# A transformer-style block on one core: the last chunk of the output projection and half of the first gate chunk done one token tile after the other

## The chip, the core and the metric

One core of a Trainium2 chip runs the whole kernel. The metric is the device time of one execution in microseconds (us), taken as the median of several runs. The engines are TensorE (PE in the rows, PEld for its weight loads), VectorE (DVE), ScalarE (ACT), GpSimd (POOL) and SyncE (SP, which here only issues transfers). L and a number is a line of the kernel.

## What is computed

One layer of a block with batch 1, 256 tokens and D_MODEL = 2048, all in float32. Three token mixers (a short gated convolution, a differential attention, a cross attention into 256 memory tokens) give `merged`; then follows what matters here:

```
x = x + rmsnorm(merged @ w_o, g_mix_post)          # w_o 2048 x 2048
h = rmsnorm(x, g_ffn_pre)
u = causal_dwconv(h @ w_up, ffn_conv_w)            # w_up 2048 x 11264
gate, val = split(u, 2)
x = x + rmsnorm((silu(gate) * val) @ w_down, g_ffn_post)
```

`rmsnorm(x, g) = x * rsqrt(mean(x*x) + 1e-6) * g`, with the mean over the 2048 channels of a token.

## The kernel before, in words

**Weights in blocks.** The 256 tokens are two token tiles of 128 (NT = 2, t = 0 and 1). All weights stream in blocks of 256 rows by 512 columns (512 KB, KB = 2 slices of 128 rows); a chunk is 512 output columns and takes CB = 8 blocks when the inner dimension is 2048. SyncE loads a block into one of RING = 4 buffers `raw`. To keep float32 accuracy each block is split in two `float32r` parts: ScalarE writes `w_hi` (a rounded copy, `split`, L434), VectorE writes `w_lo` = raw - w_hi (L696), both in rings of four. SyncE may reload a `raw` buffer when the low part of the block that was in it is written (`lo_ready`); ScalarE may overwrite a `w_hi` when TensorE has finished with the block in it (`block_done`).

**The output projection.** Four chunks of 512 columns (NCH = 4). For each block TensorE does `multiply` (L1061 to L1063): for each of 2 slices and each of 2 token tiles three matmuls of 512 columns (hi·hi, hi·lo, lo·hi), 12 in all. The tokens are the stationary side, the weights move. A chunk fills two PSUM banks, one for each token tile; `ACC[0]` is banks 0 and 1, `ACC[1]` banks 2 and 3, and the last chunk uses `ACC[1]`.

**Between the projections.** When the last chunk is done, ScalarE squares it (`mix_squares`, L598), VectorE adds the sums of squares (L970) and multiplies by the gain (`mix_out`, L915), GpSimd forms r_mix (L381, L384), VectorE writes the new x (L980) in four groups g of 512 channels, both token tiles in a group, and TensorE transposes each group (`turn`, L1075, eight transposes 128x128). From PSUM ScalarE writes `h2_hi` (L443) and VectorE `h2_lo` (L704); the two lie side by side in `h2_pair`, which the rows name hT_pair. ScalarE squares the new x (L646) for the second norm. That norm's factor is not applied to h but to the columns of the up projection: it is spread over a row of 256 tokens by two matmuls (L1261, `r_row`) and multiplied in afterwards.

**The up projection.** Eleven steps, each a gate chunk (PSUM banks 0 to 3) and a value chunk (banks 4 to 7). Here the weights are stationary and the tokens move. For each block `multiply_up` does 2 slices x 4 column blocks x 2 matmuls: L1241 multiplies a 128x128 piece of w_hi with [h2_hi | h2_lo], 512 columns, and L1243 the same piece of w_lo with h2_hi, 256 columns.

Every engine's order is written out by hand, and each runs its own list; semaphores tie them. The order around the change on ScalarE is in `up_step` (L633 to L651), on VectorE in `new_x` and `up_step` (L967 to L1009), on TensorE in L1222 to L1277.

## Time and profile before

| | |
|---|---|
| median of 3 runs | 1710.1 us (1707.93 to 1711.38) |
| time of the profiled execution | 1701.58 us |
| span of its instructions | 1699.8 us |
| mean granted TensorE clock | 0.994 |
| busy: PE, PEld, DVE, ACT, POOL | 1673.2, 1408.2, 1004.0, 799.2, 21.4 us |
| bytes moved, mean rate | 320.89 MB, 189 GB/s |

All times below are from the one profiled execution. Its time is 8.5 us under the median of the runs. A matmul's recorded duration contains its way through the array, and matmuls overlap, so the cost of one in a row of them is the distance between starts, not its duration.

### The profile page before, as it was taken

How to read it: one execution, taken by the hardware profiler on the slowest of the kernel's cores; microseconds unless marked ns; L12 is line 12 of the kernel's file. 1: busy time of each engine (PE TensorE's matmuls, PEld its weight loads, DVE VectorE, ACT ScalarE, POOL GpSimd, SP SyncE). 2: the span in 40 equal slices, each digit the busy share in tenths (PEclk: the TensorE clock that was granted, in tenths of full speed). 3: DMA queues.
4: the chain of work that ended last, by engine and by line, in shares of the span. 5: the costliest groups of instructions: out<-in, count | busy, mean ns of one | idle time of the engine just before them, and what ended most of it. 6: DMA issues, size and time to landing. Idle time of an engine off the chain costs nothing.

```text
span 1699.8 us, 23037 instructions
## 1 busy us (share of the span) xinstructions
PE 1673.2 (98%) x8201; PEld 1408.2 (83%) x8201; DVE 1004.0 (59%) x1148; ACT 799.2 (47%) x1006; POOL 21.4 (1%) x49
## 2 busy tenths in 40 slices
PE   8999999999999999999999899999999999999997
PEld 7888888888888888888888688888888888888886
DVE  5554555544556656665555567777777777644544
ACT  5544444444444444444444455555555555443442
POOL 0000000000000000000000000000000000000000
PEclk9999999999999999999999899999999999999999
DMA  7666555666655655575655356666666566655653
GB/s 275 203 177 185 170 159 163 186 187 185 191 183 194 236 184 180 179 233 193 198 191 188 119 177 193 190 187 196 186 195 187 184 183 188 234 190 170 210 198 123
DMA packets 165791, 320.89 MB, mean 189 GB/s; under 512 B 10520, under 2 KB 11369, under 8 KB 165225
## 3 DMA queue, kind: packets, MB, share of 16 engines
q1 hardware_dynamic: 165705, 320.15, 59.7%
q8 instruction: 35, 0.57, 0.1%
q14 instruction: 19, 0.16, 0.0%
q10 hardware_dynamic: 32, 0.01, 0.0%
HBM read 318.02 MB, written 2.10 MB: 188 GB/s over the span
## 4 chain that ended last, share of the span: by engine, by line
PE 95%; DVE 3%; ACT 1%; issue 1%; DMA 0%; DVEq 0%; SPq 0%; ACTq 0%
PE PS L1241 19%; PE PS L1061 18%; PE PS L1063 18%; PE PS L1062 18%; PE PS L1243 10%; PE PS L1213 3%; PE PS L1212 3%; PE PS L1211 3%; PE PS L1075 1%; ACT w_hi L434 0%; PE PS L1153 0%; PE PS L1138 0%; DMA mem_sb<-in_mem_dram 0%; DVE y_down L1043 0%; ACT p_diff L565 0%
## 5 line engine op out<-in xcount | busy, mean ns | idle before, releaser
L696 DVE TENSOR_TENSOR w_lo<-raw,w_hi 128x1024 fp32r<-128x1024 f32 x583 | 709.4, 1224 | 632.0 <-ACT w_hi L434 629.5
L434 ACT ACTIVATE w_hi<-raw 128x1024 fp32r<-128x1024 f32 x583 | 609.6, 1057 | 627.1 <-PE PS L1063 507.7
L1241 PE MATMUL PS<-hT_pair,w_hi 128*128 128x512 f32 x1408 | 489.7, 392 | 0.0
L1243 PE MATMUL PS<-hT_pair,w_lo 128*128 128x256 f32 x1408 | 394.6, 280 | 0.0
L1061 PE MATMUL PS<-w_hi,hT_pair 128*128 128x512 f32 x832 | 329.5, 396 | 0.0
L1063 PE MATMUL PS<-w_hi,hT_pair 128*128 128x512 f32 x832 | 324.3, 390 | 0.0
L1062 PE MATMUL PS<-w_lo,hT_pair 128*128 128x512 f32 x832 | 323.9, 389 | 0.0
L1241 PEld LDWEIGHTS PS<-hT_pair,w_hi 128*128 128x128 f32 x1408 | 264.0, 188 | 58.2 <-issue 0.3
L1243 PEld LDWEIGHTS PS<-hT_pair,w_lo 128*128 128x128 f32 x1408 | 266.6, 189 | 0.0
L1061 PEld LDWEIGHTS PS<-w_hi,hT_pair 128*128 128x128 f32 x832 | 156.3, 188 | 33.6 <-issue 2.7
L1063 PEld LDWEIGHTS PS<-w_hi,hT_pair 128*128 128x128 f32 x832 | 156.2, 188 | 33.1
L1062 PEld LDWEIGHTS PS<-w_lo,hT_pair 128*128 128x128 f32 x832 | 156.4, 188 | 31.3
L1061 PE MATMUL PS<-w_hi,act_hi 128*128 128x512 f32 x352 | 137.2, 390 | 0.0
L1063 PE MATMUL PS<-w_hi,act_lo 128*128 128x512 f32 x352 | 137.0, 389 | 0.0
L1062 PE MATMUL PS<-w_lo,act_hi 128*128 128x512 f32 x352 | 136.9, 389 | 0.0
L1061 PEld LDWEIGHTS PS<-w_hi,act_hi 128*128 128x128 f32 x352 | 66.1, 188 | 14.4 <-issue 0.6
L1063 PEld LDWEIGHTS PS<-w_hi,act_lo 128*128 128x128 f32 x352 | 66.1, 188 | 13.7
L1062 PEld LDWEIGHTS PS<-w_lo,act_hi 128*128 128x128 f32 x352 | 66.1, 188 | 13.6
L1061 PE MATMUL PS<-w_hi,memT_hi 128*128 128x512 f32 x128 | 51.2, 400 | 1.0 <-DVE up_taps L726 0.7
L1063 PE MATMUL PS<-w_hi,memT_lo 128*128 128x512 f32 x128 | 50.2, 392 | 0.0
L1062 PE MATMUL PS<-w_lo,memT_hi 128*128 128x512 f32 x128 | 50.2, 392 | 0.0
L1061 PE MATMUL PS<-w_hi,mixT_hi 128*128 128x512 f32 x128 | 49.9, 390 | 0.0
(185 smaller groups left out, 1280.4 us busy)
## 6 DMA issues: line engine op xcount, KB each, us to landing
raw<-in_w_up_dram SPq DMA_DIRECT2D x176, 512.0 KB, 3.8
raw<-in_w_in_dram SPq DMA_DIRECT2D x112, 512.0 KB, 3.7
raw<-in_w_gate_dram SPq DMA_DIRECT2D x96, 512.0 KB, 3.9
raw<-in_w_down_dram SPq DMA_DIRECT2D x88, 512.0 KB, 4.1
raw<-in_w_mem_kv_dram SPq DMA_DIRECT2D x32, 512.0 KB, 4.0
raw<-in_w_o_dram SPq DMA_DIRECT2D x32, 512.0 KB, 3.6
raw<-in_w_conv_out_dram SPq DMA_DIRECT2D x16, 512.0 KB, 3.6
raw<-in_w_cross_out_dram SPq DMA_DIRECT2D x16, 512.0 KB, 3.8
```

Of the source, the lines that this page charges most:

```text
L434: nc.scalar.activation(w_hi[i % RING][:], raw[i % RING][:], ACT.Copy).then_inc(hi_ready, inc)
L696: nc.vector.tensor_tensor(w_lo[i % RING][:], raw[i % RING][:], w_hi[i % RING][:].bitcast(F32), ALU.subtract).then_inc(lo_ready, inc)
L1061: nc.tensor.matmul(o, a_hi, b_hi, start=first, stop=False)
L1062: nc.tensor.matmul(o, a_hi, b_lo, start=False, stop=False)
L1063: last = nc.tensor.matmul(o, a_lo, b_hi, start=False, stop=last_k)
L1075: last = nc.tensor.transpose(dst[:, b, t * P:(t + 1) * P], src[:, t, b * P:(b + 1) * P], ident[:])
L1211: nc.tensor.matmul(ACC[1][:, t, :], hi[:, k, s], w_hi[i % RING][:, c, :], start=k == 0, stop=False)
L1212: nc.tensor.matmul(ACC[1][:, t, :], hi[:, k, s], w_lo[i % RING][:, c, :], start=False, stop=False)
L1213: last = nc.tensor.matmul(ACC[1][:, t, :], lo[:, k, s], w_hi[i % RING][:, c, :], start=False, stop=k == HK - 1)
L1241: nc.tensor.matmul(o.rearrange("p (a t) -> p a t", a=2), b_hi, h2_pair[:, :, k, :], start=k == 0, stop=False, skip_group_check=True)
L1243: last = nc.tensor.matmul(o[:, 0:TOK], b_lo, h2_hi[:, k, :], start=False, stop=last_k, skip_group_check=True)
```

## The change

The last chunk of the output projection keeps all its eight blocks (`kept_hi`, `kept_lo`: four new buffers each beside the ring of four), and TensorE goes through them twice: first all blocks for token tile 0, then all for token tile 1. Squares, gain, r_mix, the new x, its transposes and the hi/lo halves of h2 are done for one token tile at a time. The eight pieces are listed in MID as (t, g), and each has one PSUM bank of its own out of banks 4 to 7. The first gate chunk of the up projection also keeps its eight blocks. Its blocks 0 to 3 (SPLIT = 4) are multiplied for token tile 0 (column blocks 0 to 2 first, since bank 3 still holds the output projection's tile 1) and later for token tile 1; blocks 4 to 7 for both together as before. Transposes stand between those pieces.

```diff
+SPLIT = 4
+MID = [(0, 0), (0, 1), (1, 0), (1, 1), (0, 2), (1, 2), (0, 3), (1, 3)]
...
+        kept_hi = [at(f"kept_hi{s}", RD + 16 * K + 4 * K * s, [P, KB, CW], F32R) for s in range(RING)] + w_hi
+        kept_lo = [at(f"kept_lo{s}", RD + 44 * K + 4 * K * s, [P, KB, CW], F32R) for s in range(RING)] + w_lo
...
+        MID_T = [PS[:, 4 + p % 4, :].rearrange("p (b t) -> p b t", t=P) for p in range(len(MID))]
...
-            pool.wait_ge(mix_sum, 1)
-            rms(r_mix[:], sq_mix[:], D)
+            for t in range(NT):
+                pool.wait_ge(mix_sum, t + 1)
+                rms(r_mix[:, t:t + 1], sq_mix[:, t:t + 1], D, 1)
...
+            def split_kept(n, i, fresh=False):
+                act.wait_ge(raw_in[i % RING], 4 * n + 16 * (i // RING + 1))
+                if not (fresh and i < RING):
+                    act.wait_ge(block_done, n + i - 2 * RING + 1)
+                nc.scalar.activation(kept_hi[i][:], raw[i % RING][:], ACT.Copy).then_inc(hi_ready, 1)
...
+            def last_squares(t):
+                if t == 0:
+                    act.wait_ge(o_first, 1)
+                else:
+                    act.wait_ge(block_done, N_UP)
+                act.wait_ge(mix_sq, NT * (NCH - 1) + 2 * t)
+                nc.scalar.activation(junk[:], ACC[1][:, t, :], ACT.Square, accum_out=sq_part[:, t, NCH - 1:NCH]).then_inc(mix_sq, 1)
+            def new_squares(t):
+                act.wait_ge(x_new, NCH * (t + 1))
+                act.wait_ge(mix_sq, NT * (NCH - 1) + 1 + 2 * t)
+                nc.scalar.activation(junk_wide[:], x_res[:, t, :], ACT.Square, accum_out=sq_h2[:, t:t + 1]).then_inc(mix_sq, 1)
+            def middle_hi(p):
+                t, g = MID[p]
+                act.wait_ge(mid_turned, p + 1)
+                for b in range(BPC):
+                    k = BPC * g + b
+                    last = nc.scalar.activation(h2_hi[:, k, t * P:(t + 1) * P], MID_T[p][:, b, :], ACT.Copy, scale=g_ffn_v[:, k:k + 1])
+                last.then_inc(mid_hi, 1)
+            def middle():
+                last_squares(0)
+                split_kept(N_UP, 0)
+                split_kept(N_UP, 1)
+                split_kept(N_UP, 2)
+                middle_hi(0)
+                split_kept(N_UP, 3)
+                middle_hi(1)
+                split_kept(N_UP, 4)
+                split_kept(N_UP, 5)
+                new_squares(0)
+                last_squares(1)
+                split_kept(N_UP, 6)
+                middle_hi(2)
+                middle_hi(3)
+                split_kept(N_UP, 7)
+                for p in range(4, 8):
+                    middle_hi(p)
+                new_squares(1)
+                act.wait_ge(r_row_turned, 1)
+                nc.scalar.activation(r_row[:], PS[:, 4, 0:TOK], ACT.Copy).then_inc(r_row_done, 1)
...
+            def last_out(t):
+                s = slice((NCH - 1) * CW, NCH * CW)
+                dve.wait_ge(mix_sq, NT * (NCH - 1) + 1 + 2 * t)
+                nc.vector.tensor_reduce(sq_mix[:, t:t + 1], sq_part[:, t, :], AX.X, ALU.add).then_inc(mix_sum, 1)
+                nc.vector.tensor_tensor(y_mix[:, t, s], ACC[1][:, t, :], g_post[:, s], ALU.mult).then_inc(mix_last, 1)
+            def new_x(t, g):
+                if g == 0:
+                    dve.wait_ge(mix_last, t + 1)
+                    dve.wait_ge(xres_in, 16 * NT)
+                    dve.wait_ge(rms_ready, 3 + t)
+                s = slice(g * CW, (g + 1) * CW)
+                nc.vector.scalar_tensor_tensor(out=x_res[:, t, s], in0=y_mix[:, t, s], scalar=r_mix[:, t:t + 1],
+                                               in1=x_res[:, t, s], op0=ALU.mult, op1=ALU.add).then_inc(x_new, 1)
+            def middle_lo(p):
+                t, g = MID[p]
+                dve.wait_ge(mid_hi, p + 1)
+                for b in range(BPC):
+                    k, s = BPC * g + b, slice(t * P, (t + 1) * P)
+                    last = nc.vector.scalar_tensor_tensor(out=h2_lo[:, k, s], in0=MID_T[p][:, b, :], scalar=g_ffn_v[:, k:k + 1],
+                                                          in1=h2_hi[:, k, s].bitcast(F32), op0=ALU.mult, op1=ALU.subtract)
+                last.then_inc(mid_lo, 1)
+            def middle():
                 dve.wait_ge(evacuated[0], E_UP)
-                dve.wait_ge(xres_in, 16 * NT)
-                dve.wait_ge(rms_ready, 3)
-                for g in range(NCH + 1):
-                    if g < NCH:
-                        s = slice(g * CW, (g + 1) * CW)
-                        for t in range(NT):
-                            last = nc.vector.scalar_tensor_tensor(out=x_res[:, t, s], in0=y_mix[:, t, s], scalar=r_mix[:, t:t + 1],
-                                                                  in1=x_res[:, t, s], op0=ALU.mult, op1=ALU.add)
-                        last.then_inc(x_new, 1)
-                    if g:
-                        prepare(2 * NCH + g - 1, g - 1, (SCORE_T, TURN)[(g - 1) % 2], g_ffn_v, h2_hi, h2_lo)
+                dve.wait_ge(evacuated[1], E_UP - 1)
+                last_out(0)
+                new_x(0, 0)
+                new_x(0, 1)
+                split_kept(N_UP, 0)
+                split_kept(N_UP, 1)
+                middle_lo(0)
+                new_x(0, 2)
+                new_x(0, 3)
+                split_kept(N_UP, 2)
+                middle_lo(1)
+                split_kept(N_UP, 3)
+                last_out(1)
+                split_kept(N_UP, 4)
+                new_x(1, 0)
+                new_x(1, 1)
+                split_kept(N_UP, 5)
+                middle_lo(2)
+                middle_lo(3)
+                new_x(1, 2)
+                new_x(1, 3)
+                split_kept(N_UP, 6)
+                middle_lo(4)
+                middle_lo(5)
+                split_kept(N_UP, 7)
+                middle_lo(6)
+                middle_lo(7)
                 dve.wait_ge(mix_sq, NT * NCH + NT)
                 nc.vector.tensor_copy(sq_mix[:], sq_h2[:]).then_inc(h2_sq, 1)
+                dve.wait_ge(rms_ready, 5)
+                nc.vector.memset(ones[:], 1.0)
+                for t in range(NT):
+                    last = nc.vector.tensor_scalar(r_diag[:, t, :], ident[:], r_h2[:, t:t + 1], None, ALU.mult)
+                last.then_inc(r_diag_done, 1)
...
+            def middle_turn(p):
+                t, g = MID[p]
+                if p == 0:
+                    pe.wait_ge(turned_read, T_UP)
+                if p >= 4:
+                    pe.wait_ge(mid_lo, p - 3)
+                pe.wait_ge(x_new, NCH * t + g + 1)
+                for b in range(BPC):
+                    c0 = (BPC * g + b) * P
+                    last = nc.tensor.transpose(MID_T[p][:, b, :], x_res[:, t, c0:c0 + P], ident[:])
+                last.then_inc(mid_turned, 1)
+            def last_chunk():
+                n, acc = N_O + CB * (NCH - 1), ACC[1]
+                pe.wait_ge(evacuated[1], E_O + 1)
+                for t in range(NT):
+                    s = slice(t * P, (t + 1) * P)
+                    for i in range(CB):
+                        if t == 0:
+                            pe.wait_ge(lo_ready, n + i + 1)
+                        for c in range(KB):
+                            k = KB * i + c
+                            b_hi, b_lo = kept_hi[i][:, c, :], kept_lo[i][:, c, :]
+                            nc.tensor.matmul(acc[:, t, :], mixT_hi[:, k, s], b_hi, start=k == 0, stop=False)
+                            nc.tensor.matmul(acc[:, t, :], mixT_hi[:, k, s], b_lo, start=False, stop=False)
+                            last = nc.tensor.matmul(acc[:, t, :], mixT_lo[:, k, s], b_hi, start=False, stop=k == DK - 1)
+                        if t:
+                            last.then_inc(block_done, 1)
+                        elif i == CB - 1:
+                            last.then_inc(o_first, 1)
+                        if t and i in (3, 4):
+                            middle_turn(i - 3)
+            def first_gate():
+                def tile(i, t, blocks):
+                    s = slice(t * P, (t + 1) * P)
+                    for c in range(KB):
+                        k = KB * i + c
+                        for b in blocks:
+                            w = slice(b * P, (b + 1) * P)
+                            o = UP[0][:, b, :].rearrange("p (a t) -> p a t", a=2)
+                            nc.tensor.matmul(o[:, :, s], kept_hi[i][:, c, w], h2_pair[:, :, k, s], start=k == 0 and t == 0, stop=False,
+                                             skip_group_check=True)
+                            last = nc.tensor.matmul(o[:, 0, s], kept_lo[i][:, c, w], h2_hi[:, k, s], start=False, stop=False,
+                                                    skip_group_check=True)
+                    return last
+                pe.wait_ge(evacuated[0], E_UP)
+                pe.wait_ge(mix_last, 1)
+                for i in range(SPLIT):
+                    pe.wait_ge(mid_lo, i // 2 + 1)
+                    pe.wait_ge(lo_ready, N_UP + i + 1)
+                    tile(i, 0, range(BPC - 1))
+                    if i >= 2:
+                        middle_turn(i)
+                pe.wait_ge(mix_last, 2)
+                for i in range(SPLIT):
+                    tile(i, 0, range(BPC - 1, BPC))
+                middle_turn(4)
+                for i in range(SPLIT):
+                    pe.wait_ge(mid_lo, 2 + i // 2 + 1)
+                    tile(i, 1, range(BPC)).then_inc(block_done, 1)
+                    if i < 3:
+                        middle_turn(5 + i)
+                for i in range(SPLIT, CB):
+                    pe.wait_ge(mid_lo, 6 if i // 2 == 2 else 8)
+                    multiply_up(N_UP, i, 0, kept_hi[i], kept_lo[i])
+                    if i == CB - 2:
+                        spread_scale()
```

Beside this the squares and gain product of the third output chunk come two blocks later in the last chunk (after block 5, not 3), and `new_x`, `prepare` and the transposes of before are gone from this stage. How the orders differ:

TensorE, around the end of the output projection. Before, all transposes of the new x (x_res) stand together behind the last output matmul (L1063) and ahead of the first up matmul (L1241); the names in brackets are the semaphores waited for:

```order
L1063 MATMUL PS<-w_hi3_56,mixT_lo_102 128x512
L1075 MATMUL PS<-ident_61,x_res_106 128x128 [waits x_new]
L1075 MATMUL PS<-ident_61,x_res_106 128x128 x7
L1075 MATMUL PS<-ident_61,x_res_106 128x128 [waits x_new,turned_read]
L1075 MATMUL PS<-ident_61,x_res_106 128x128 x7
L1075 MATMUL PS<-ident_61,x_res_106 128x128 [waits x_new,prep_lo]
L1075 MATMUL PS<-ident_61,x_res_106 128x128 x7
L1075 MATMUL PS<-ident_61,x_res_106 128x128 [waits x_new,prep_lo,turned_read]
L1075 MATMUL PS<-ident_61,x_res_106 128x128 x7
L1241 MATMUL PS<-hT_pair_92,w_hi0_53 128x512 [waits prep_lo,lo_ready,evacuated1,evacuated0]
```

In the changed kernel the third piece of transposes, which is token tile 1's first, stands between block 2 and block 3 of the gate chunk; L1363 is the hi matmul of one token tile (2x128 columns), L1365 the lo matmul (128 columns):

```order
L1363 MATMUL PS<-hT_pair_92,kept_hi2_140 128x2x128
L1365 MATMUL PS<-hT_pair_92,kept_lo2_144 128x128
L1329 MATMUL PS<-ident_61,x_res_106 128x128 [waits x_new]
L1329 MATMUL PS<-ident_61,x_res_106 128x128 x3
L1363 MATMUL PS<-hT_pair_92,kept_hi3_141 128x2x128 [waits lo_ready,mid_lo]
L1365 MATMUL PS<-hT_pair_92,kept_lo3_145 128x128
```

What moved: 32 transposes that stood in one place are eight pieces of four among matmuls, and a 512/256 pair of columns has become two pairs of 256/128.

ScalarE, the same stage before, from the squares of the last chunk to the next splits of weights:

```order
L598 ACTIVATE junk_137,sq_part_78<-PS 128x512 [waits mix_sq,block_done]
L598 ACTIVATE junk_137,sq_part_78<-PS 128x512 [waits mix_sq]
L443 ACTIVATE hT_pair_92<-PS,vecs_63 128x256 [waits prep_turned]
L443 ACTIVATE hT_pair_92<-PS,vecs_63 128x256 x3
L443 ACTIVATE hT_pair_92<-PS,vecs_63 128x256 [waits prep_turned]
L443 ACTIVATE hT_pair_92<-PS,vecs_63 128x256 x3
```

ScalarE in the changed kernel, from block 3 of the gate chunk on (L614 splits a block, L648 writes a piece of h2_hi, L640 squares the whole new x of token tile 0, L634 squares the last chunk of token tile 1):

```order
L614 ACTIVATE kept_hi3_141<-raw3_52 128x1024 [waits block_done,raw_in3]
L648 ACTIVATE hT_pair_92<-PS,vecs_63 128x128 [waits mid_turned]
L648 ACTIVATE hT_pair_92<-PS,vecs_63 128x128 x3
L614 ACTIVATE w_hi0_53<-raw0_49 128x1024 [waits block_done,raw_in0]
L614 ACTIVATE w_hi1_54<-raw1_50 128x1024 [waits block_done,raw_in1]
L640 ACTIVATE junk_wide_146,sq_h2_80<-x_res_106 128x2048 [waits mix_sq,x_new]
L634 ACTIVATE junk_137,sq_part_78<-PS 128x512 [waits mix_sq,block_done]
L614 ACTIVATE w_hi2_55<-raw2_51 128x1024 [waits block_done,raw_in2]
```

What moved: token tile 1's squares (L634) now stand behind five weight splits and the long squares of token tile 0.

VectorE in the changed kernel, from token tile 1's sum of squares to its transposed halves (L1032 adds the sums, L1033 multiplies by the gain, L965 writes a low part of weights, L1042 writes a group of the new x, L1051 a piece of h2_lo):

```order
L1032 TENSOR_REDUCE sq_mix_79<-sq_part_78 128x1 [waits mix_sq]
L1033 TENSOR_TENSOR y_mix_110<-PS,g_post_117 128x512
L965 TENSOR_TENSOR w_lo0_57<-raw0_49,w_hi0_53 128x1024 [waits hi_ready]
L1042 SCALAR_TENSOR_TENSOR x_res_106<-y_mix_110,r_mix_75,x_res_106 128x512 [waits rms_ready,xres_in,mix_last]
L1042 SCALAR_TENSOR_TENSOR x_res_106<-y_mix_110,r_mix_75,x_res_106 128x512
L965 TENSOR_TENSOR w_lo1_58<-raw1_50,w_hi1_54 128x1024 [waits hi_ready]
```

Before, the same place holds all of the last chunk at once, and no weights:

```order
L970 TENSOR_REDUCE sq_mix_79<-sq_part_78 128x2 [waits mix_sq]
L915 TENSOR_TENSOR y_mix_110<-PS,g_post_117 128x512 [waits mix_sq]
L915 TENSOR_TENSOR y_mix_110<-PS,g_post_117 128x512
L980 SCALAR_TENSOR_TENSOR x_res_106<-y_mix_110,r_mix_75,x_res_106 128x512 [waits xres_in,rms_ready,evacuated0,evacuated1]
L980 SCALAR_TENSOR_TENSOR x_res_106<-y_mix_110,r_mix_75,x_res_106 128x512 x3
```

What moved: a weight's low part now stands between the gain product and the new x of token tile 1.

## Rows read from the trace of the kernel before

**Rows 1.** The page's first part: busy time of TensorE and its share of the span.
```profile
PE 1673.2 (98%) x8201; PEld 1408.2 (83%) x8201; DVE 1004.0 (59%) x1148; ACT 799.2 (47%) x1006; POOL 21.4 (1%) x49
```
**Rows 2.** Stretches between the projections: busy PE, PEld, DVE, ACT, POOL, then PEclk, DMA share, GB/s.
```profile
944.00:948.00 4.00, 0.04 (x1) 0.00 (x0) 2.45 (x5) 1.38 (x4) 0.88 (x2) 1.00 0.51 155
948.00:951.00 3.00, 2.62 (x13) 2.62 (x14) 1.65 (x3) 0.62 (x2) 0.00 (x0) 0.50 0.00 0
951.00:954.50 3.50, 0.90 (x6) 0.70 (x6) 3.25 (x7) 2.41 (x7) 0.00 (x0) 0.95 0.00 0
958.00:961.50 3.50, 3.50 (x14) 3.11 (x13) 2.08 (x6) 2.25 (x5) 0.00 (x0) 0.50 0.02 5
962.00:966.00 4.00, 4.00 (x25) 3.48 (x25) 0.30 (x2) 3.94 (x6) 0.81 (x2) 1.00 0.00 0
```
**Rows 3.** TensorE in order of time: start us, us, line, [idle before it <- releaser].
```profile
943.65 0.39 PE L1063 MATMUL PS<-w_hi,mixT_lo 128*128 128x512 f32 x1
...
948.38 3.41 PE L1075 MATMUL PS<-ident,x_res 128*128 128x128 f32 x16 [4.34 <-DVE x_res L980]
...
954.38 1.57 PE L1075 MATMUL PS<-ident,x_res 128*128 128x128 f32 x8 [2.60 <-DVE x_res L980]
...
957.27 1.94 PE L1075 MATMUL PS<-ident,x_res 128*128 128x128 f32 x8 [1.32 <-DVE x_res L980]
...
958.86 0.77 PE L1241 MATMUL PS<-hT_pair,w_hi 128*128 128x512 f32 x1
...
959.65 0.63 PE L1241 MATMUL PS<-hT_pair,w_hi 128*128 128x512 f32 x1
...
960.29 0.63 PE L1241 MATMUL PS<-hT_pair,w_hi 128*128 128x512 f32 x1
```
**Rows 4.** TensorE at full clock: transposes, the scale's matmuls, up pairs, first value matmul.
```profile
861.39 1.03 PE L1075 MATMUL PS<-ident,stage 128*128 128x128 f32 x8
...
979.63 0.60 PE L1261 MATMUL PS<-r_diag,ones 128*128 128x128 f32 x4
...
980.77 0.39 PE L1241 MATMUL PS<-hT_pair,w_hi 128*128 128x512 f32 x1
981.00 0.28 PE L1243 MATMUL PS<-hT_pair,w_lo 128*128 128x256 f32 x1
981.12 0.39 PE L1241 MATMUL PS<-hT_pair,w_hi 128*128 128x512 f32 x1
...
983.01 0.47 PE L1241 MATMUL PS<-hT_pair,w_hi 128*128 128x512 f32 x1
```
**Rows 5.** Output projection by tile: durations ns min/median/max, first and last start us.
```profile
L1061 PE MATMUL PS<-w_hi,mixT_hi x128: 389/389/476, 855.9 to 943.2; 128*128 128x512 f32 x128
```
**Rows 6.** The other engines between the projections, in order of time.
```profile
944.07 0.60 ACT L598 ACTIVATE junk<-PS 128x512 f32<-128x512 f32 x1 [1.60 <-PE PS L1063]
...
945.51 0.16 DVE L970 TENSOR_REDUCE sq_mix<-sq_part 128x2 f32<-128x8 f32 x1 [1.78 <-ACT junk L598]
945.59 1.28 DVE L915 TENSOR_TENSOR y_mix<-PS,g_post 128x512 f32<-128x512 f32 x2
...
946.04 0.69 POOL L384 TENSOR_TENSOR r_mix<-mean_sq,minus_half 128x2 f32<-128x2 f32 x1
946.91 2.74 DVE L980 SCALAR_TENSOR_TENSOR x_res<-y_mix,r_mix,x_res 128x512 f32<-128x512 f32 x4
...
954.15 1.65 DVE L704 SCALAR_TENSOR_TENSOR hT_pair<-PS,vecs,hT_pair 128x256 fp32r<-128x256 f32 x4
...
955.99 1.57 ACT L443 ACTIVATE hT_pair<-PS,vecs 128x256 fp32r<-128x256 f32 x4 [2.58 <-PE PS L1075]
...
960.69 1.93 ACT L646 ACTIVATE junk_wide<-x_res 128x2048 f32<-128x2048 f32 x1
...
964.78 2.96 ACT L434 ACTIVATE w_hi<-raw 128x1024 fp32r<-128x1024 f32 x3
...
965.87 2.36 DVE L696 TENSOR_TENSOR w_lo<-raw,w_hi 128x1024 fp32r<-128x1024 f32 x2 [0.92 <-ACT w_hi L434]
```
**Rows 7.** DMA issues: size and median us from issue to landing.
```profile
raw<-in_w_up_dram SPq DMA_DIRECT2D x176, 512.0 KB, 3.8
```

109 lines of the change are left out of this document (45 added, 64 removed).

## The prediction

> **What bounds the kernel now.** I read the page first. TensorE is busy 98% of the span [rows 1], so time can only come from the places where it stands still or runs slowly. I then cut the span into stretches and looked for those where PE's busy time or its granted clock drops. One such place lies where this change is made: in 944 to 948 us TensorE is busy 0.04 us of 4.00, in 948 to 951 us and again in 958 to 961.5 us its clock is 0.50 (1.2 GHz instead of 2.4), and from 962 us on it is full again [rows 2].
>
> The time order says why. The last output matmul starts at 943.65, the first transposes at 948.38 after 4.34 us idle, and two more waits of 2.60 and 1.32 us follow, all three released by VectorE's new x (L980); the first up matmul starts at 958.86 [rows 3]. Behind the 4.34 us stands a chain over all engines: squares at 944.07, sum at 945.51, gain product at 945.59, r_mix at 946.04, new x from 946.91 [rows 6].
>
> How much is lost there? At full clock:
> - an output matmul costs 0.2275 us. From the first L1061 at 855.9 to the last at 943.2 there are 127 steps of three, with eight transposes (0.9 us) among them: (87.3 - 0.9) / 381 = 0.227 [rows 5];
> - an up pair of 512 and 256 columns costs 0.348 us: two starts at 980.77 and 981.12, of which the 512-column one takes 0.23 and the 256-column one 0.115 [rows 4];
> - a transpose costs (1.03 - 0.27) / 7 = 0.109 us, if 0.27 is one's own duration, and each of the four records that the two scale matmuls leave (0.60 - 0.27) / 3 = 0.11, so 0.22 a matmul [rows 4].
>
> From the end of the last output matmul, 943.65 + 0.23 = 943.88, to the first value matmul at 983.01 [rows 3, 4] it is 39.1 us. The work in it is 64 pairs (22.25), 32 transposes (3.5) and the two scale matmuls (0.4), 26.1 us. So **13.0 us are lost**: 8.3 waiting, and 4.7 since most transposes and the first four pairs ran at half clock (a pair then takes 0.64, 959.65 to 960.29 [rows 3]). 13.0 us is 0.8% of the kernel and the most that this change can give.
>
> **The change part by part.** All sums count from the end of the last output matmul of token tile 0, or of both.
>
> *The output chunk in two passes.* 96 matmuls of 512 columns before and after: 0. The second pass (48 matmuls, 10.9 us, with two pieces of transposes between, 11.9) is what covers tile 0's chain. That its blocks are all there in the first pass needs eight blocks held: four go to new buffers without waiting for TensorE, so they are split during the third chunk; nothing waits. With that cover gone a block would cost the landing time, 3.8 us [rows 7].
>
> *Tile 0's chain.* Durations come from the rows of before, halved where one token tile is done: squares to +0.9 us, sum +1.0, gain product (half of 1.28) +1.65, r_mix +2.1, first new x (2.74 / 4 = 0.69) +2.9 [rows 6]. TensorE asks for it after four blocks of the second pass, 24 x 0.2275 = +5.5. Hidden with 2.6 us to spare. h2's first piece: transposes done at +6.1, four ScalarE copies, four VectorE operations. Of 128 columns I have no row. 256 columns take 1.57 / 4 = 0.39 on ScalarE and 1.65 / 4 = 0.41 on VectorE [rows 6]. The slope from there to 1024 columns on ScalarE (2.96 / 3 = 0.99) and to 512 on VectorE (0.69) gives 0.29 and 0.28 for 128; the upper bound is no saving at all. So the piece is ready at +8.5 and TensorE wants it at +11.9. Hidden. Thus the 4.34 us wait goes completely.
>
> *Tile 1's chain: here is the one wait left.* Let 0 be the end of the first pass, so tile 1 is done at 11.9. Its squares could start at 12.1, but on ScalarE they stand behind the splits of blocks 3, 4 and 5 (0.99 each), two pieces of copies (1.2 each) and the squares of the whole tile 0 (2.07 with its read-out). In order: first piece 6.1 to 7.3, block 3 to 8.3, second piece to 9.4, blocks 4 and 5 to 11.4, long squares to 13.5, tile 1's squares to 14.2. The raw blocks 4 and 5 are asked for at 5.0 and 6.2 and land 3.8 us later [rows 7], in time. VectorE then has the sum (0.1), the gain product (0.64), the low part of block 4 (2.36 / 2 = 1.18), and the first new x (0.69): 16.9. TensorE has three blocks of three column pieces to do from 11.9, 18 narrow pairs. At 0.231 a pair (below) that is 4.16, to 16.05. It waits **0.9 us**, for VectorE's x_res. The next thing that can be late is the third group of tile 1's new x, needed at 23.5 and there at 22.5, so nothing. The last pieces (hi7, lo7) are done 10 us before blocks 6 and 7 need them, and the second norm's factor 4 us before the scale matmuls.
>
> *Narrow matmuls: the cost that the change adds.* Blocks 0 to 3 took 32 pairs of 512/256 columns; now they are 64 pairs of 256/128. If cost went by columns this would be free. But each pair loads its two weights again. 256 columns cost 0.115. For 128 columns of this type the trace has no row. The bounds: 0.057, half of 256; and 0.22, what a plain float32 matmul of 128 columns costs in its two records [rows 4]. I take **0.115, the same as 256 columns**: no two starts with a weight load between them are nearer than 0.109 in these rows. Then 64 x 0.231 = 14.8 against 32 x 0.348 = 11.1: **+3.65 us**. The ends: 64 x 0.173 = 11.1 (+0, but then TensorE asks 1.05 us earlier and waits that much longer, so +1), and 64 x 0.335 = 21.4 (+10.3, and the wait of 0.9 is gone).
>
> The Trainium skill has two rules here (TensorE: Matmul & The Clock Gate). Its section on the back-to-back gap gives a lone 128-column matmul N / 2.4 + 2.5, about 56 ns, the low end; its section on LDWEIGHTS gives a weight load of 128 columns about 107 ns whatever the contraction. By the first alone the sum would be some 2.7 us better, by the second 0.5 better. The 0.109 of the rows speaks for the second, but comes from another type of matmul.
>
> *Transposes.* 32 before and after, at full clock 3.5 us. Eight places instead of four, and after eight transposes the next matmul starts in the rows about 0.05 late; 8 x 0.05 = +0.4.
>
> *The end of the stage.* The value chunk's first block still cannot be split before the row of scales is read by ScalarE, as before; that small stop is inside the 39.1 us, and I allow 0.1 us for it again. More loops, semaphores and GpSimd's two small norms instead of one are beside other work.
>
> **The sum.** 26.1 + 3.65 + 0.4 + 0.9 + 0.1 = 31.1 us instead of 39.1: **8.0 us less**. The profiled execution would go from 1701.6 to 1693.6; against the median of 1710.1 that is **1702.1 us** (-0.47%). What can be told from no change here is about 0.2%, 3.4 us.
>
> **The rivals.**
> 1. *128-column float32r matmuls cost as much as plain float32, 0.22.* For it: plain float32 is the only 128-column multiplication in the trace, and it costs that. Against it: 256 and 512 columns of this type cost in proportion to their columns, so the type by itself is not slow. The stage is then 26.1 + 10.3 + 0.4 + 0.1 = 36.9, so 2.2 us less, 1707.9: within 0.2%.
> 2. *The chains are longer than my slopes.* If 128 columns cost ScalarE and VectorE what 256 do, the wait at tile 1's first transposes grows from 0.9 to 1.8 us and a small one of 0.1 follows; gain 7.0, 1703.1. Landings 3 us late on top would put blocks 4 and 5, which stand ahead of the squares on ScalarE, late by about as much: gain 4 to 5, still faster.
> 3. *Slower: the clock falls and stays at 1.2 GHz through the tiled stretch.* The stretch has a wait of 0.9 us, transposes in eight places and narrow matmuls. At half clock a narrow pair costs 0.21 + 0.21, if 128 columns again go like a transpose of that stretch (3.41 us for 16 with three at the end faster [rows 3], 0.21 each): 64 x 0.43 = 27.3 instead of 14.8, and six pieces of transposes 2.5 more, less the wait: +14. That is 6 us slower than before, 1716. It decides once the half clock covers more than 8/14 of some 18 us, so 10 us. Against it: the clock was still 1.00 over the 4 us without work, 944 to 948, and fell only behind them [rows 2]; a wait of 0.9 us is far from that. The skill says (same page, PE-mode transpose) that transposes do not count as activity for the full clock. That rule would be this rival's reason. The rows say otherwise: 948 to 951 us holds nothing but transposes at 0.50, and 951 to 954.5 us stands at 0.95 [rows 2].
>
> **How the numbers follow.** My forecast, with rival 2 as its own upper part, 0.68 (of this rival 2 is 0.12): gain 4 to 10, that is 1700 to 1706. Rival 1: 0.21, 1706.5 to 1709. Rival 3: 0.06. The rest, 0.05, is some wait I have not seen, of either sign. The low end takes the gain of 10 with narrow pairs at 0.173 and 1 us of scatter between runs (the three of before lie 3.5 apart): 1699. The high end has to reach into rival 1 to hold 8 in 10: 1708.5. Faster by over 0.2%: 0.71; within 0.2%: 0.22; slower by over 0.2%: 0.07.
>
> **What the profile after would show.** The 4.34 us wait is gone, and the largest left on TensorE in this stage is about 0.9 us, before the transposes of token tile 1's first group, released by x_res. The distance between two starts of L1363 is 0.23; 0.17 or 0.33 would show my price for 128 columns wrong. The clock stays at 1.00 from the output projection into the up projection. From the first matmul of the last output chunk to the first value matmul it takes 53 us (before: 21.8 + 39.1 = 60.9). If these hold and the time doesn't fall, a later stage has given the gain back, which I see no reason for: from the first value chunk on the order is the same and TensorE sets the pace. I am wrong above all if the narrow pairs take over 0.30 us, or if TensorE shows a second wait of over 2 us.

## The result, and the profile after

| | before | changed |
|---|---|---|
| median | 1709.77 us (1707.93 to 1711.38, 4 executions) | 1692.06 us (1691.04 to 1692.9, 4 executions) |
| profiled execution | 1701.58 us | 1691.04 us |
| span | 1699.8 us | 1689.2 us |
| mean granted TensorE clock | 0.994 | 0.998 |

The ratio is 0.9911, 95% interval 0.9884 to 0.9937: 17.7 us less. The forecast was 8.0 us less, at 1702.1 us, and its range ended at 1699.0. So the time is outside the range. Already here two numbers don't fit each other: between the medians there are 17.7 us, between the profiled executions 10.5. The kernel before's profiled execution, 1701.58, is none of its four timed ones and lies over 6 us under the lowest of them.

The page's first part of the changed kernel, which answers to [rows 1]:

```profile
PE 1670.8 (99%) x8265; PEld 1408.2 (83%) x8265; DVE 1005.0 (59%) x1165; ACT 801.4 (47%) x1022; POOL 22.0 (1%) x51
```

Stretches of the changed kernel between the projections (us, busy PE, PEld, DVE, ACT, POOL, then PEclk, DMA share, GB/s), against [rows 2]:

```profile
930.00:942.00 12.00, 12.00 (x59) 9.94 (x58) 8.36 (x15) 8.72 (x16) 0.74 (x2) 1.00 0.27 89
942.00:947.00 5.00, 4.92 (x40) 4.65 (x38) 3.82 (x8) 3.95 (x6) 0.74 (x2) 1.00 0.66 188
947.00:950.00 3.00, 2.39 (x21) 2.39 (x22) 2.88 (x5) 1.14 (x4) 0.00 (x0) 1.00 0.67 184
950.00:961.00 11.00, 11.00 (x99) 10.96 (x98) 9.21 (x26) 7.42 (x22) 0.00 (x0) 1.00 0.50 143
961.00:973.00 12.00, 12.00 (x71) 10.44 (x70) 2.92 (x8) 4.41 (x7) 0.89 (x2) 1.00 0.03 10
```

The clock column is 1.00 in every row; in [rows 2] it was 0.50 in two of them. TensorE is idle for 0.08 + 0.61 = 0.69 us in 43 us.

TensorE of the changed kernel in order of time, against [rows 3] and the value chunk's start in [rows 4]. L1346 is the last output matmul, L1363 and L1365 are the narrow pair, L1420 and L1422 the 512/256 pair:

```profile
942.42 0.39 PE L1346 MATMUL PS<-w_hi,mixT_lo 128*128 128x512 f32 x1
942.64 0.28 PE L1363 MATMUL PS<-hT_pair,kept_hi 128*128 128x256 f32 x1
942.76 0.22 PE L1365 MATMUL PS<-hT_pair,kept_lo 128*128 128x128 f32 x1
942.82 0.34 PE L1363 MATMUL PS<-hT_pair,kept_hi 128*128 128x256 f32 x1
942.99 0.22 PE L1365 MATMUL PS<-hT_pair,kept_lo 128*128 128x128 f32 x1
943.05 0.34 PE L1363 MATMUL PS<-hT_pair,kept_hi 128*128 128x256 f32 x1
...
947.61 0.66 PE L1329 MATMUL PS<-ident,x_res 128*128 128x128 f32 x4 [0.70 <-DVE x_res L1042]
...
971.63 0.40 PE L1420 MATMUL PS<-hT_pair,w_hi 128*128 128x512 f32 x1
971.87 0.28 PE L1422 MATMUL PS<-hT_pair,w_lo 128*128 128x256 f32 x1
971.98 0.40 PE L1420 MATMUL PS<-hT_pair,w_hi 128*128 128x512 f32 x1
972.22 0.28 PE L1422 MATMUL PS<-hT_pair,w_lo 128*128 128x256 f32 x1
972.45 0.47 PE L1420 MATMUL PS<-hT_pair,w_hi 128*128 128x512 f32 x1
972.76 0.28 PE L1422 MATMUL PS<-hT_pair,w_lo 128*128 128x256 f32 x1
972.88 0.39 PE L1420 MATMUL PS<-hT_pair,w_hi 128*128 128x512 f32 x1
973.11 0.28 PE L1422 MATMUL PS<-hT_pair,w_lo 128*128 128x256 f32 x1
973.22 0.39 PE L1420 MATMUL PS<-hT_pair,w_hi 128*128 128x512 f32 x1
```

The first up matmul follows the last output matmul after 0.22 us; before it took 15.2 us, 943.65 to 958.86 [rows 3]. One wait is left, 0.70 us, before token tile 1's first transposes. The chain behind it on ScalarE and VectorE of the changed kernel, which answers to [rows 6]:

```profile
942.21 1.90 ACT L640 ACTIVATE junk_wide<-x_res 128x2048 f32<-128x2048 f32 x1
...
944.29 0.60 ACT L634 ACTIVATE junk<-PS 128x512 f32<-128x512 f32 x1
...
945.01 0.16 DVE L1032 TENSOR_REDUCE sq_mix<-sq_part 128x1 f32<-128x4 f32 x1 [1.18 <-ACT junk L634]
945.08 0.68 DVE L1033 TENSOR_TENSOR y_mix<-PS,g_post 128x512 f32<-128x512 f32 x1
945.68 1.21 DVE L965 TENSOR_TENSOR w_lo<-raw,w_hi 128x1024 fp32r<-128x1024 f32 x1
946.81 1.41 DVE L1042 SCALAR_TENSOR_TENSOR x_res<-y_mix,r_mix,x_res 128x512 f32<-128x512 f32 x2
```

Tile 1's product ends at 942.42 + 0.23 = 942.65, but its squares start only at 944.29, behind the long squares of tile 0: that delay and the low part of a weight (945.68) stand ahead of the new x, and TensorE waits for it. The view counts 0.70 us of idle, from the end that it models for the last matmul. By starts, the transposes come 0.92 us after L1365's last start (946.70 to 947.61), where 0.06 is usual, so the wait costs 0.86.

**Where the time went.** I cut both spans at two places that both kernels have: the first matmul of the last output chunk and the first value matmul. Between them it is 60.89 us before (922.12 to 983.01) and 52.51 after (919.94 to 972.45): 8.4 us. The rest of the 10.6 us between the two spans is there already long before the change. The first 25 us of the kernel before:

```profile
0.00:25.00 25.00, 20.58 (x97) 17.39 (x98) 11.80 (x19) 10.53 (x19) 0.73 (x7) 0.93 0.83 287
```

and of the changed kernel:

```profile
0.00:25.00 25.00, 21.19 (x111) 18.01 (x112) 12.04 (x20) 11.56 (x20) 0.72 (x7) 1.00 0.86 299
```

In its profiled execution the kernel before started up with a lower clock (0.93) and 14 fewer matmuls, in code that is the same in both; it is 2.2 us later at the eight transposes of x_sb (49.25 against 47.05) and at 920 us still. 8.4 + 2.2 = 10.6. This start-up scatters from execution to execution: over all 14 profiled ones of this study the last output chunk begins between 919.87 and 922.93 us, in no order of the kernels, and the two latest have a clock of 1.00 in the first 25 us, so the clock alone doesn't explain it. So the stage gives what was forecast, 8.4 against 8.0 us. Of the 17.7 us between the medians 9.3 are not the stage, and 7.1 are not in these two executions at all.

### The profile page after: what moved, and what is told of

Same layout as the page of the kernel before. It is cut to its first block, busy times and chain, and to the rows that moved or that the text cites. A ratio compares the mean times of both kernels' runs of the same rounds, so it can differ in the third digit from the quotient of the medians.

```text
span 1689.2 us, 23203 instructions
## 1 busy us (share of the span) xinstructions
PE 1670.8 (99%) x8265; PEld 1408.2 (83%) x8265; DVE 1005.0 (59%) x1165; ACT 801.4 (47%) x1022; POOL 22.0 (1%) x51
## 4 chain that ended last, share of the span: by engine, by line
PE 95%; DVE 2%; ACT 1%; issue 1%; DMA 1%; DVEq 0%; SPq 0%; POOL 0%; ACTq 0%
PE PS L1420 19%; PE PS L1158 18%; PE PS L1160 18%; PE PS L1159 18%; PE PS L1422 10%; PE PS L1310 3%; PE PS L1309 3%; PE PS L1308 3%; PE PS L1172 1%; ACT w_hi L442 0%; PE PS L1363 0%; PE PS L1250 0%; PE PS L1235 0%; DMA mem_sb<-in_mem_dram 0%; DVE y_down L1140 0%
## 5 line engine op out<-in xcount | busy, mean ns | idle before, releaser
L750 DVE TENSOR_TENSOR w_lo<-raw,w_hi 128x1024 fp32r<-128x1024 f32 x567 | 689.7, 1224 | 615.3 <-ACT w_hi L442 613.0
L442 ACT ACTIVATE w_hi<-raw 128x1024 fp32r<-128x1024 f32 x567 | 593.1, 1057 | 608.0 <-PE PS L1160 488.7
L1420 PE MATMUL PS<-hT_pair,w_hi 128*128 128x512 f32 x1376 | 477.4, 391 | 0.0
L1422 PE MATMUL PS<-hT_pair,w_lo 128*128 128x256 f32 x1376 | 385.3, 280 | 0.0
L1420 PEld LDWEIGHTS PS<-hT_pair,w_hi 128*128 128x128 f32 x1376 | 257.3, 187 | 56.6 <-issue 0.2
L1422 PEld LDWEIGHTS PS<-hT_pair,w_lo 128*128 128x128 f32 x1376 | 260.1, 189 | 0.0
L679 ACT ACTIVATE up_scaled_sb<-PS 128x1024 f32<-128x1024 f32 x22 | 22.6, 1025 | 37.6 <-PE PS L1422 37.6
```

Of the source, the lines that this page charges most:

```text
L442: nc.scalar.activation(w_hi[i % RING][:], raw[i % RING][:], ACT.Copy).then_inc(hi_ready, inc)
L679: nc.scalar.activation(up_scaled_sb[:], UP_A[half], ACT.Copy).then_inc(up_copied, 1)
L750: nc.vector.tensor_tensor(w_lo[i % RING][:], raw[i % RING][:], w_hi[i % RING][:].bitcast(F32), ALU.subtract).then_inc(lo_ready, inc)
L1420: nc.tensor.matmul(o.rearrange("p (a t) -> p a t", a=2), b_hi, h2_pair[:, :, k, :], start=k == 0, stop=False, skip_group_check=True)
L1422: last = nc.tensor.matmul(o[:, 0:TOK], b_lo, h2_hi[:, k, :], start=False, stop=last_k, skip_group_check=True)
```

## The experiments

**The theories.** The letters are those of this section; the expectations use their own. *A:* the kernel before runs in two ways, one some 8.5 us longer than the other; its profiled execution was of the short kind and all four timed ones of the long kind, and the change, by whatever mechanism, leaves only the short kind. *B:* the clock: the changed kernel is rid of a stretch at 1.2 GHz [rows 2], and the later part runs at a better clock for it. *C:* scatter: chips and start-up differ, and nothing stands behind the 9 us. The kernels ran in three groups (1 to 4, 5 to 8, 9 to 12), each on a chip of its own; a ratio is against the kernel before on the same chip. *Stage* is the time from the first matmul of the last output chunk to the first value matmul in the profiled execution.

**1. before_again.** The kernel before, unchanged.

> The kernel before, unchanged, timed against itself. The executions that gave the median of 1709.8 us are 8 us above the profiled one of 1701.6, which I did not account for. Theory A (the gap is a state of the execution, and it sits between the projections): spans around 1708 us with a mean granted clock under the 0.994 of the profiled execution, 0.985 to 0.990. Theory B (the gap lies at the start or in single transfers, and has nothing to do with the stage): clock 0.994 in all, spans scattered from 1700 to 1710 us. Theory C: the profiled execution was the exception, and times repeat at 1708 to 1711 us at a clock of 0.994. Ratio 1.000 in all three.

Measured: median 1701.32 us over 12 executions, ratio 0.9995 (0.9972 to 1.0017). Ten lie between 1700.65 and 1702.43, two at 1709.35 and 1711.23, none between. All 100 executions of the kernel before in this study fall so, with none between 1703.0 and 1707.8 us: in the upper cluster are 4 of the 4 of the result, 2 of these 12, and 10 of 27, 24 of 34 and 9 of 23 of those that ran beside the three groups, 49 of 100. Both clusters occur on each of the three chips, and the median of the lower one is 1701.0, 1701.3 and 1701.2 us there, so the chip hardly matters. C falls, and the first half of A holds: "1710.1" was the upper cluster alone. None of the expectation's three theories had it: the clocks are 0.992 to 0.995 whichever the cluster, and the times are neither scattered evenly nor all above 1708. It also means that a ratio against the kernel before depends on how many of its executions fell in either cluster; the clusters are what can be compared.

**2. after_again.** The changed kernel, unchanged.

> The changed kernel, unchanged, again. The stage itself went from 39.1 to 30.8 us in the two profiled executions, 8.3 us. If the gain is only that, medians differ by 8 to 11 us and the ratio is 0.994 to 0.995. If the slow executions of before have to do with the clock falling in the stage, the ratio stays at 0.990 to 0.992 (17 us) and the changed kernel shows a clock of 0.998 and hardly any scatter in all its executions.

Measured: 1692.67 us (1692.22 to 1693.88, 9 executions), ratio 0.9931 (0.9906 to 0.9955); stage 52.44 us, against 60.74 in before_again. One cluster. Against the lower cluster of the kernel before, 1701.3, it is 8.6 us less: the stage's 8.3 and little else. The ratio of 0.9931 lies a little under the 0.994 to 0.995 expected of the stage alone, since 10 of the 27 executions of the kernel before were in the upper cluster.

What differs between the clusters is then found by counting pairs in a stretch in which TensorE never waits. Of the changed kernel, 1000 to 1400 us, its 512-column matmuls (count, busy us, mean ns):

```profile
L1420 PE MATMUL PS<-hT_pair,w_hi 128*128 128x512 f32 x1155 | 400.4, 391 | 0.0
```

The profiled kernel before has 1155 too. 400 / 1155 = 0.346 us a pair. The next experiment has the other number.

**3. before_filled.** The kernel before, with 32 matmuls of the identity (into a free bank, read by nobody) put ahead of the four groups of transposes, so that the clock can't fall.

```diff
...
+            def fill(count):
+                for _ in range(count):
+                    nc.tensor.matmul(PS[:, 0, 0:P], ident[:], ident[:], start=True, stop=True)
+            pe.wait_ge(evacuated[0], E_UP)
             for g in range(NCH):
+                fill((18, 0, 10, 4)[g])
```

> The kernel before, with 32 plain float32 matmuls of the identity (128 columns, into a PSUM bank that nothing reads) put into the three waits between the projections: 18, 10 and 4, so that TensorE is busy while it waits for the new x. The results are not touched. Clock theory: the transposes and the first up pairs run at 2.4 GHz, the stage goes from 39.1 to 35 or 36 us in the profile, and if the clock's fall is also what the slow executions share, the median falls by more, 10 to 13 us (ratio 0.992 to 0.994). Waits-only theory: the clock is not what costs here, and the time moves by less than 1.5 us (ratio 0.999 to 1.001).

Measured: 1706.05 us (1696.67 to 1709.43, 12 executions), ratio 0.9998 (0.9972 to 1.0023). Three lie at 1696.67 to 1699.21, nine at 1705.64 to 1709.43: both clusters moved down by about 3 us, with more executions in the upper one. The ratio of 0.9998 looks like the expectation's waits-only theory, but only because nine of twelve fell in the upper cluster. The stage is 58.35 us, 2.5 less than before (3 to 4 were expected), and the clock is 1.00 all through it:

```profile
948.00:951.00 3.00, 3.00 (x28) 2.81 (x25) 2.71 (x6) 2.45 (x7) 0.00 (x0) 1.00 0.00 0
```

Its profiled execution has a span of 1704.1 us, the upper cluster. TensorE of it in 1000 to 1400 us:

```profile
L1241 PE MATMUL PS<-hT_pair,w_hi 128*128 128x512 f32 x1134 | 400.7, 399 | 0.0
```

21 pairs fewer in 400 us at a granted clock of 1.00: 0.353 us a pair. B falls, since the clock was mended and the clusters stayed. And here is the mechanism of A: two rhythms. By starts, a pair takes 347 ns in one (230 from the 512-column matmul to the 256-column one, 117 to the next) and 353 ns in the other (about 236 and 117, repeated in the order 120, 236, 113, 232, 118, 241). The 347 ns come in two forms: in before_again as 231, 112, 233, 117, 231, 113, 232, 118, with the same mean. From the first value chunk to the end of the up projection there are 21 chunks of 64 pairs; 1344 x 6.67 ns = **9.0 us**, the distance between the clusters (8.5 to 10.3 between their medians on the three chips). In the traces of the two kernels the rhythm doesn't change within that stretch. No execution of the unchanged kernel before from its upper cluster was profiled; that it has the 353 ns rhythm is concluded from this one and from experiment 5's, both in the upper cluster of kernels that differ by one small edit, and from the 9.0 us.

**4. after_squares_first.** The changed kernel, with token tile 1's squares ahead of the long squares of tile 0 on ScalarE.

```diff
...
                 split_kept(N_UP, 5)
-                new_squares(0)
                 last_squares(1)
+                new_squares(0)
                 split_kept(N_UP, 6)
```

(The counts that the semaphore mix_sq is compared with follow the new order.)

> The changed kernel with two operations of ScalarE exchanged: the squares of the last chunk for token tile 1 stand ahead of the squares of the whole new x of tile 0. My chain says that the 0.7 us wait of TensorE ahead of tile 1's first transposes goes away (the squares end 1.3 us earlier), so the stage is 0.7 us shorter than in the changed kernel: too little for the timed runs to tell, and to be seen in the profile. Rival: the wait stays, since the weight's low part and the new x on VectorE set it; then the profile shows 0.5 us or more at the same place.

Measured: 1691.8 us (1691.28 to 1692.03, 7 executions), ratio 0.9925 (0.9897 to 0.9954); stage 51.61 us, 0.9 less than the changed kernel. TensorE at the place of the wait:

```profile
947.86 0.22 PE L1365 MATMUL PS<-hT_pair,kept_lo 128*128 128x128 f32 x1
947.92 0.62 PE L1329 MATMUL PS<-ident,x_res 128*128 128x128 f32 x4
```

The wait is gone, and the stage is shorter by what it cost by starts. Tile 1's first new x starts 2.9 us after tile 1's product (946.71 after 943.81) instead of 4.2. So ScalarE's order is enough to explain the wait, as the forecast had it. VectorE's low part still stands ahead of the new x (945.58 here); whether taking it away would also have been enough was not run.

**What picks the rhythm?** Two interruptions stand ahead of the long row of pairs, and there the traces show the rhythm change: the two scale matmuls ahead of the gate chunk's last block, and a stop of 0.1 us before the first value matmul, whose block ScalarE splits only after it has read the row of scales. In the changed kernel's rows above, the last pairs of the gate chunk start 0.35 apart and 0.24 after 971.63 comes the 256-column matmul (the 353 ns rhythm); the starts 972.22 and 972.45 are 0.23 apart instead of 0.12, which is the stop; and from 972.88 on it is 0.23 to the 256-column matmul and 0.34 to the next pair (the 347 ns rhythm). The traces hold more of this. In all eight profiled executions with the tiled gate chunk (the changed kernel three times, and experiments 4, 6, 8, 10 and 11) the gate's pairs run at 347 ns up to the scale matmuls and at 353 behind them. In the six with the gate chunk whole the rhythm behind the scale matmuls is 347 in five and 353 in one. So in every profile of it the changed kernel comes to the value chunk in the 353 ns rhythm, and needs the stop to leave it. The next four kernels change this place.

**5. before_value_early.** The kernel before, with the value chunk's first block split before the row is read, so that there is no stop.

```diff
                     elif i == CB - 1:
+                        split(n, CB)
                         act.wait_ge(r_row_turned, 1)
...
-                    split(n, CB + i)
+                    if i or jp is not None:
+                        split(n, CB + i)
```

> The kernel before with one exchange on ScalarE: the high part of the first value block of the first up step is written ahead of the row of scales, so TensorE need not wait for the low part when it begins the value chunk. Direct effect on the stage: 0.1 to 0.2 us. The profiles so far show the ten later up steps in three rhythms: a pair of 512 and 256 columns every 0.3467 us (steps 230 and 117 ns, or a longer pattern with the same mean) or every 0.3533 us (120, 236, 113, 232, 118, 241 ns), which makes 9 us over 1340 pairs, and the rhythm never changes once the value chunk has begun. Restart theory: the rhythm is picked when TensorE starts again at the value chunk, so a start without the wait gives all executions the same rhythm; if the fast one, median 1701 us with nothing over 1704. Stage theory (the rhythm depends on what lies ahead, the idle time or the clock): about a third of the executions stay at 1708 to 1712 us.

Measured: 1704.83 us (1698.41 to 1711.58, 12 executions), ratio 0.9979 (0.9958 to 0.9999); six in each cluster. In the profiled one the 353 ns rhythm of the last gate blocks goes on through the value chunk without a break. Without a stop the rhythm isn't fixed, it is inherited. So the expectation's restart theory misses in the form it was given (one rhythm for all), and its rival, a third in the upper cluster, is nearer. The stage of the profiled one is 61.29 us, not shorter than before.

**6. after_value_late.** The changed kernel, with TensorE made to wait ahead of the value chunk until its first two blocks are split, not only the first.

```diff
                     pe.wait_ge(r_row_done, 1)
+                    pe.wait_ge(lo_ready, N_UP + CB + 2)
```

> The changed kernel with one more wait on TensorE: it begins the value chunk of the first up step only when the low part of the second value block is there, some 1.2 us later, since VectorE writes one block in 1.2 us. Direct cost 1.1 to 1.3 us (1693.8 us). Restart theory: the moment of the restart decides the rhythm, so another moment can bring the slow one (0.3533 us a pair) into some or all executions, 1702 to 1703 us. Stage theory: the changed stage is what keeps the rhythm fast, and all executions stay at 1693 to 1695 us.

Measured: 1702.41 us (1693.33 to 1704.08, 12 executions), ratio 0.9957 (0.9936 to 0.9978): three at 1693.33 to 1693.59, nine at 1701.1 and above. Stage 53.64 us. TensorE at the stop of the profiled one, which is of the nine:

```profile
973.98 0.28 PE L1422 MATMUL PS<-hT_pair,w_lo 128*128 128x256 f32 x1
975.30 0.47 PE L1420 MATMUL PS<-hT_pair,w_hi 128*128 128x512 f32 x1 [1.04 <-DVE w_lo L750]
975.61 0.28 PE L1422 MATMUL PS<-hT_pair,w_lo 128*128 128x256 f32 x1
975.72 0.40 PE L1420 MATMUL PS<-hT_pair,w_hi 128*128 128x512 f32 x1
...
976.07 0.40 PE L1420 MATMUL PS<-hT_pair,w_hi 128*128 128x512 f32 x1
...
976.43 0.40 PE L1420 MATMUL PS<-hT_pair,w_hi 128*128 128x512 f32 x1
```

A wait that costs 1.1 us in the stage costs 9.7 in the median (against experiment 2's, on another chip). A longer stop alone brings the upper cluster into the changed kernel. That the changed kernel's own short stop picks the 347 ns rhythm, A's second half, is shown at the place, and experiment 8 takes the stop away.

**7. after_whole_gate.** The changed kernel, with the gate chunk whole: only the output chunk is done tile by tile.

```diff
-                for i in range(SPLIT):
...
-                    tile(i, 0, range(BPC - 1))
...
+                for p in range(2, 5):
+                    middle_turn(p)
+                for i in range(CB):
+                    pe.wait_ge(mid_lo, (3, 4, 6, 8)[i // 2])
+                    multiply_up(N_UP, i, 0, kept_hi[i], kept_lo[i])
```

> Half of the change alone: the last output chunk in two passes with its chain by token tile, but the first gate chunk whole, all eight blocks with 512 and 256 columns, after the transposes of token tile 1 have begun. TensorE then has nothing to do from the end of the output chunk to tile 1's new x. My schedule gives the first up pair 8.1 us after the last output matmul and the stage (first matmul of the last output chunk to first value matmul) 55.0 us, 2.4 more than the changed kernel's, and up to 2 us more if the clock falls in the 5 us without work: 57 at most. That would leave about 4 to 6 us of the 8.4 us gain to the chunk's split and 2.4 to 4.4 us to the gate's. Rival: the narrow matmuls' 3.65 us eat all that the tiled gate covers, and this kernel is as fast as the changed one (52.5 us).

Measured: 1705.92 us (1696.65 to 1708.43, 12 executions), ratio 0.9979 (0.9958 to 0.9999): again two clusters, four at 1696.65 to 1698.82 and the rest at 1702.98 and 1705.63 to 1708.43. TensorE of the profiled one:

```profile
948.79 2.58 PE L1329 MATMUL PS<-ident,x_res 128*128 128x128 f32 x12 [4.80 <-DVE x_res L1042]
952.06 0.79 PE L1396 MATMUL PS<-hT_pair,kept_hi 128*128 128x512 f32 x1 [0.69 <-DVE hT_pair L1051]
```

and its 949 to 952 us:

```profile
949.00:952.00 3.00, 2.37 (x12) 1.87 (x10) 2.57 (x7) 2.30 (x9) 0.00 (x0) 0.51 0.79 195
```

The stage is 56.99 us, the upper end of what was expected (55 to 57). Of the change's 8.4 us the output chunk's tiles by themselves give 3.9 (three waits of 8.3 us together have become two of 5.5), and the gate chunk's tiles 4.5: with no narrow pairs to cover it, tile 1's chain is a wait of 4.80 us, and the clock behind it is 0.51 in 949 to 952 us. The other engines keep the changed kernel's order here, so this splits the gain for this order, not for the best one that a whole gate chunk could have.

**8. after_best.** The two shorter orders together: squares first as in 4, value block early as in 5.

```diff
                 split_kept(N_UP, 5)
-                new_squares(0)
                 last_squares(1)
+                new_squares(0)
                 split_kept(N_UP, 6)
...
                 new_squares(1)
+                split(N_UP, CB)
                 act.wait_ge(r_row_turned, 1)
...
```

(And the rest of both edits, as in 4 and 5.)

> The changed kernel with both exchanges on ScalarE: token tile 1's squares ahead of the long squares, and the first value block's high part ahead of the row of scales. Stage: 0.7 us less by the first, 0.1 us by the second against the changed kernel; 1691.6 us if the rhythm is the fast one. If a start without a wait picks the slow rhythm, 1700 us.

Measured: 1700.95 us (1698.86 to 1701.97, 11 executions), ratio 0.9961 (0.9943 to 0.998). The stage is the shortest of all, 51.49 us, and the kernel is 9 us longer than the one with squares first alone. Its 512-column matmuls in 1000 to 1400 us (the lines are two later here):

```profile
L1422 PE MATMUL PS<-hT_pair,w_hi 128*128 128x512 f32 x1133 | 400.4, 399 | 0.0
```

and TensorE around the first value matmul, 974.42:

```profile
974.07 0.40 PE L1422 MATMUL PS<-hT_pair,w_hi 128*128 128x512 f32 x1
974.31 0.28 PE L1424 MATMUL PS<-hT_pair,w_lo 128*128 128x256 f32 x1
974.42 0.40 PE L1422 MATMUL PS<-hT_pair,w_hi 128*128 128x512 f32 x1
974.66 0.28 PE L1424 MATMUL PS<-hT_pair,w_lo 128*128 128x256 f32 x1
974.78 0.40 PE L1422 MATMUL PS<-hT_pair,w_hi 128*128 128x512 f32 x1
```

No stop, and the gate chunk's 353 ns rhythm is kept for 9 us' worth of pairs. This is the clearest of the experiments: beside kernel 4 only one split on ScalarE stands elsewhere, which takes away the stop of 0.1 us, and the median is 9.2 us higher, in all 11 executions. The two ran on different chips, but kernel 4 gave 1691.8 and 1691.67 us on two chips, and the chips' lower clusters of the kernel before lie 0.3 us apart.

**9. after_chip2.** The changed kernel again, on another chip.

> The changed kernel once more, on another chip, since the kernel before showed the slow rhythm in 10 of 27 executions on one chip and in 24 of 34 on another. Restart theory (block 7 of the gate chunk always ends in the same rhythm, and the short stop at the value chunk, 234 ns between starts, always brings the fast one): all executions at 1692 to 1694 us again. If the rhythm is a matter of the chip or of chance in each execution, some lie at 1701 to 1703 us.

Measured: 1693.19 us (1691.05 to 1694.03, 6 executions), ratio 0.9925 (0.9895 to 0.9955), stage 52.61 us. All 19 executions of the changed kernel are in the lower cluster.

**10. squares_first_chip2.** Kernel 4 again, on that chip.

> The changed kernel with token tile 1's squares ahead of tile 0's long squares, once more. It keeps the stop at the value chunk. By the restart theory again all executions in the fast rhythm, 0.7 to 1.0 us below the changed kernel: 1691 to 1692 us. This is the candidate for a version faster than both.

Measured: 1691.67 us (1690.29 to 1692.41, 6 executions), ratio 0.9916 (0.9887 to 0.9946). On both chips its median is below the changed kernel's, by 0.9 and 1.5 us; the stage is 51.61 us on both, 0.8 to 1.0 less. On the first chip all its executions are under all of the changed kernel's, on the second they overlap. It is the best version found.

**11. after_best_nudged.** Kernel 8, with one small matmul before each value chunk, to see whether the rhythm is picked anew each time.

```diff
                     pe.wait_ge(up_summed, 2 * jp + 2)
+                nc.tensor.matmul(PS[:, 4, 0:16], ident[:], ident[:, 0:16], start=True, stop=True)
```

> The kernel with both exchanges on ScalarE, which ran all eleven executions in the slow rhythm (median 1700.95 us), plus one small matmul (16 columns of the identity, overwritten at once) ahead of the value chunk of every up step, so the row of pairs is interrupted 11 times. Direct cost under 0.2 us each, 2 us at most. Theory that any interruption lets the rhythm be picked anew: the profile shows chunks of both rhythms, or only the fast one, and the median lies between 1692 and 1699 us. Rival (only a stop for a semaphore does that): the slow rhythm in every chunk, 1701 to 1703 us.

Measured: 1698.81 us (1697.07 to 1700.36, 12 executions), ratio 0.9969 (0.995 to 0.9988), 1138 pairs in the 400 us. The starts of the small matmul show what it does. One stands ahead of each value chunk, so 128 pairs lie between two of them:

```profile
971.36 0.29 PE L1439 MATMUL PS<-ident 128*128 128x16 f32 x2
...
1016.81 0.29 PE L1439 MATMUL PS<-ident 128*128 128x16 f32 x2
...
1061.42 0.29 PE L1439 MATMUL PS<-ident 128*128 128x16 f32 x2
...
1106.87 0.29 PE L1439 MATMUL PS<-ident 128*128 128x16 f32 x2
...
1151.47 0.29 PE L1439 MATMUL PS<-ident 128*128 128x16 f32 x2
```

The distances are 45.45, 44.61, 45.45 and 44.60 us and alternate so to the end; 0.85 us is 128 x 6.67 ns. Read pair by pair, every step holds one rhythm throughout, 353.3, 346.7, 353.3, 346.7 ns and so on. So the nudge doesn't pick a rhythm at random: from the second one on, each of the ten flips it to the other. Only the first, which stands where the stop of the changed kernel was, leaves the 353 ns of the gate chunk. The time follows: 11 of the 21 chunks at 353 ns are 4.7 us, 11 nudges at 0.23 us (0.2 was expected at most) are 2.5, and 1691.7 + 4.7 + 2.5 = 1698.9. The flips also rule out the clock, the chip and anything else that lasts for a whole execution as the cause of the rhythm, since one execution goes back and forth between the two.

**12. before_nudged.** The same line in the kernel before.

> The kernel before with the same small matmul ahead of each value chunk. If an interruption picks the rhythm anew, the two clusters of before (1698 to 1703 and 1708 to 1712 us) melt into one, with a spread of under 4 us and a median between them; if the rhythm comes only from the first value chunk's stop, both clusters stay, 1 to 2 us higher.

Measured: 1707.52 us (1705.7 to 1709.21, 12 executions), ratio 1.001 (0.9992 to 1.0029). The two clusters are one, 3.5 us wide. The nudges start at 981.36, 1025.97, 1071.42, 1116.02 and 1161.47 us, so 44.61, 45.45, 44.60 and 45.45 apart: the same alternation, beginning with 346.7 ns. No execution keeps one rhythm to the end, half of the pairs run in either, and the clusters are gone with it. Again the sum fits: ten chunks at 353 ns are 4.3 us and the nudges 2.5, on 1701.2 that is 1708.0.

## Why the prediction was wrong, step by step

**The step that failed** is the last one of the sum: "against the median of 1710.1 that is 1702.1 us". It took the 8.5 us between the median and the profiled execution over to the changed kernel as if they were a constant. The gap was that of two kinds of execution of the kernel before, one with 353 ns a pair and one with 347 (9.0 us in 1344 pairs), and the changed kernel doesn't have the longer one: 8.4 from the stage + 9.0 = 17.4 of the measured 17.7. The range failed with it; it held 1 us of "scatter between runs", where the kernel itself has two clusters. (Its low end takes a gain of 10, where its own terms give 8.0 + 3.65 - 1.05 = 10.6; that would not have reached the measured time either.) The forecast for the profiled execution, 1693.6, is 2.6 us from 1691.04, of which 2.2 are the start-up; it is 0.9 us from experiment 2's median, 1692.67.

**What was the draw.** The size of the miss is partly chance. All four timed executions of the kernel before fell in the upper cluster; of the 96 later ones 45 did, so if each falls by itself, four of four happens about once in twenty. Had they fallen in the lower one, the same change would have measured 8.6 us less, next to the forecast of 8.0. Against the 27 and 23 executions on two chips, the changed kernel's medians are 9.6 and 9.1 us lower (0.9931 and 0.9925). What is not chance is that the changed kernel has one cluster only, 19 of 19; that it is the lower one the forecast had no term for.

**The bound.** 13.0 us to be had at most in the stage, 8.3 waiting and 4.7 clock. Held: TensorE is at 1.00 throughout. Of the clock's part: with the clock alone mended (experiment 3) the stage gave 2.5 us, not 4.7. The two traces show where the rest stays, counted from the start of the last output matmul. The first transposes start after 4.73 us in both. The third group starts after 9.86 instead of 10.73 and the first up pair after 13.57 instead of 15.21; the first pairs at full clock give another 0.9. So the transposes that end sooner wait again for a new x that comes only 0.9 us earlier. before_again shows the same from the other side: its clock is at 0.50 to 0.54 from 948 to 961 us, without the 0.95 of [rows 2] between, and its stage is no longer (60.74).

**The two passes and tile 0's chain:** hidden, as said; no wait before the second pass's transposes, and the 4.34 us of [rows 3] are gone. **Tile 1's chain:** 0.9 us forecast; 0.70 of idle in the view, 0.86 by starts, and 0.8 to 0.9 by taking it away (experiment 4), at the place and with the releaser named. The x was ready 4.9 us after tile 1's product (forecast 5.0: 16.9 - 11.9). The order of what makes it late was right too (experiment 4). The second possible wait, the third group, didn't come.

**The narrow pair:** 0.231 us forecast, 0.230 measured (64 pairs, start to start, 942.82 to 943.05 is one). But the working behind it was off in its parts: not 0.115 for 128 columns, but 0.06 from L1365's start to the next and 0.17 from L1363's. What is nearly constant is the distance between weight loads. TensorE's weight loads in the changed kernel:

```profile
942.99 0.19 PEld L1363 LDWEIGHTS PS<-hT_pair,kept_hi 128*128 128x128 f32 x1
943.10 0.19 PEld L1365 LDWEIGHTS PS<-hT_pair,kept_lo 128*128 128x128 f32 x1
943.22 0.19 PEld L1363 LDWEIGHTS PS<-hT_pair,kept_hi 128*128 128x128 f32 x1
943.33 0.19 PEld L1365 LDWEIGHTS PS<-hT_pair,kept_lo 128*128 128x128 f32 x1
```

Over all the narrow pairs they start 0.107 to 0.128 apart, 0.115 on average, where the matmuls' starts go 0.17 and 0.06: I read the pair as two weight loads, whatever the 384 columns would need. The Trainium skill (TensorE: Matmul & The Clock Gate, section on LDWEIGHTS) has about 107 ns for a load of 128 columns; by the distance of starts the trace agrees to 8 ns (the records themselves last 0.19 us), and its figure for a lone 128-column matmul, 56 ns (section on the back-to-back gap), is not the one that counts here. Rival 1 (0.22) is excluded.

**Turns:** +0.4 forecast; a piece of four takes 0.37 us from its start to the next pair (947.92 to 948.29 in experiment 4), and that pair is 0.03 longer; together 0.40, below 4 x 0.109, so nothing was added. **The sum:** 52.9 us from the first matmul of the last output chunk to the first value matmul (the text rounds to 53), measured 52.51; the 0.4 of the turns is about the difference.

**Rival 3, the clock:** it stayed at 1.00 over narrow pairs, eight pieces of transposes and the 0.70 us wait. In after_whole_gate it fell, behind a wait of 4.80 us, as in [rows 2] behind 4.34. Two details of that rival don't hold. That the clock "was still 1.00 over the 4 us without work" is one execution: in before_again it is 0.86 over the same 944 to 948 us. And the 0.95 behind nothing but transposes, on which it leans too, is one execution as well: in before_again the same transposes are followed by 0.50 in 951 to 955 us. Its 64 x 0.43 is 27.5, not 27.3, which changes nothing.

**What stays open:** which detail of an interruption picks the rhythm. The changed kernel's stop picks 347 ns in 19 of 19 (squares first: 13 of 13), the same stop made 1 us longer picks it in 3 of 12, the kernel before in 51 of 100. The effect and its places are shown, and so is that a small matmul in the row flips the rhythm; why it flips, and a rule that would forecast the outcome of a stop, are not. A single nudge in kernel 8, which might turn its 353 ns into 347, was not run.

## What to carry to other kernels

Before a forecast is set against a median, look at whether the profiled execution lies in it: a gap of 0.5% is a finding to be explained, not an offset to carry over. In long rows of matmuls count pairs in a stretch without waits, in each profile; a per cent can hide there at full clock and with nothing idle. And where an edit takes away or moves a small stop ahead of such a row, time a dozen executions, since the stop's own 0.1 us is not what it is worth. Compare clusters, not medians, where a kernel has two: the median of four executions can be that of one cluster alone.

## What the runs showed of the hardware

- **A row of matmuls with weight loads has more than one steady rhythm** at a granted clock of 1.00: 347 and 353 ns for 512 + 256 columns of float32r, 1.9% apart. It is set where the row is interrupted and is then kept for hundreds of microseconds (experiments 3, 5, 6, 8). An added matmul of 16 columns in the running row costs 0.23 us and flips it to the other rhythm, 10 times out of 10 in each of two kernels (11, 12).
- **A pair of 256 + 128 columns takes two weight loads,** 0.230 us, though 384 columns would fit into less: half of the 512/256 pair's 0.347 is 0.173.
- **Filling the waits with 32 identity matmuls** kept the clock at 1.00, and took 2.5 us off the stage.
